# A projection stage with split fp32r products instead of fp32 ones, and the top-k selection spread along it

## Chip, cores and metric

One core of one Trainium2 chip runs the whole program in one launch. The metric is the device time of one execution in microseconds (us). "PE" is TensorE, "DVE" VectorE, "ACT" ScalarE, "POOL" GpSimd, and "SP" the queue that issues the DMAs.

## The reference, cut to what matters

Two request groups (1024 prompt frames and 32 sample frames, 1056 tokens in all) pass through two layers. Each layer normalises x, projects it with one wide `w_in`, runs four attention groups (sb, df, ds, fx), an output projection and a gated MLP with a depthwise convolution. The change is in the input projection and in what chooses the keys of the sparse group ds:

```python
hn = rmsnorm(x, g_mix)
parts = split_proj(jnp.einsum('btd,dn->btn', hn, w_in))      # 1024 -> 12 x 256 (q, k, v of 4 groups), 8*64 + 64 + 8 index columns, 4 gates
s_ix  = relu(einsum('bqhd,bkd->bqhk', q_ix, k_ix) * 64**-0.5)  # 8 index heads, one shared index key
score = einsum('bqh,bqhk->bqk', w_ix * 8**-0.5, s_ix)
score = where(chunk_ok, score, -inf)
top_val, top_idx = lax.top_k(score, topk)                      # topk = 256 for the prompt, 40 for the sample
logf  = log_sigmoid(parts[15] + b_forget);  c_all = cumsum(cat(plogf, logf))
```

The k and v rows, the index keys and `logf` are also outputs.

## The kernel before

Everything is a hand-written schedule: each stage is a `phase` in which five engine programs run side by side, tied by counted semaphores, and all engines meet at a barrier at its end. SBUF is one tensor, `arena`, that stages carve up anew. A loop over the two layers runs the stages in this order: norm, project the index columns, project the groups and select, attend, norm with the output projection in it, MLP.

**Norm** (`stage_norm`). xT holds x feature-major, 8 chunks of 128 features by 1056 tokens, and the norm goes in three pieces of 352 tokens. Called for the projection it writes the normalised values to hT by 24 DVE operations (line 565). Called with `split=True` (so far only ahead of the MLP) it writes them to a ring, ACT rounds each to fp32r (line 456), and DVE subtracts the rounded value to get the rest (line 534): `h_split` then holds a high and a low part.

**Index projection** (`stage_project_index`). For each of 9 token tiles (8 of 128 and one of 32) PE multiplies hT by the 584 index columns (line 650, plain fp32), ACT copies the result, PE turns it to feature-major (line 641) and DVE keeps it as qixT and kixT (lines 685, 687). kixT holds the shared key twice, with zeros in the other 64 rows, so that one product with all 128 rows picks one head of a pair.

**Projection and selection** (`stage_project_select`). 36 tiles (4 groups, GROUP_ORDER, by 9 token tiles) of 768 or 772 columns: products at line 883, ACT's copy to `nat` (line 942), the turns of q and k (line 898), their scaled copies (lines 952, 953) and the stores. Beside it, for the sample block (160 keys, "block 8") and the six prompt blocks with 384 to 1024 keys ("blocks 2 to 7"; the two smaller ones need no selection), PE makes the index scores of a head (line 907, two PSUM banks in turn), ACT applies the relu (line 969, a ring of 6), DVE multiplies by the head's weight and adds (lines 1012, 1014), masks the last tile of keys (line 1019) and then takes the largest 8 and marks them, 32 times in a row (5 for the sample; lines 1022, 1023). A last operation turns the marks into flags times 1e30 (line 1026). `projection_plan` puts the scores of a block among the tiles: `part 0` (the first 6 units) about one tile ahead, `part 1` when the block is due. Since each engine runs its program in order, PE, ACT and SP all follow that one list.

At block 5 stands the cumulative sum of the gates (`gates`, lines 991 and 996), for which PE turns the log gates (line 923).

**Attend** reads the flags as an fp32r operand of a product that adds them to the logits (line 1269), and starts with the queries and keys that the stage before wrote to DRAM (`q_turned`, `k_turned`).

Of the kernel before, what the change touches and what calls it, by code (L numbers as in the profile page):

```python
# [25 lines left out]
Unit = namedtuple("Unit", "v st heads map0 last")  # L26
Turn = namedtuple("Turn", "i kind of a t0 tiles eng nth")
# [23 lines left out]
RELU_RING = 6  # L51
# [15 lines left out]
WIDTH = dict(sb=3 * GW, df=3 * GW, ds=3 * GW, ix=NIX * HD + HD + NIX, fx=3 * GW + NH)  # L67
MIX = dict(sb=0, df=2, ds=4, fx=6)
W_OUT_SLOT = dict(ds=0, df=1, fx=0, sb=1)
PROJ = COL["fx"] + WIDTH["fx"]  # L70
# [13 lines left out]
BLOCKS = query_blocks()  # L84
TILES = [(i, i * P, P) for i in range(NT)] + [(NT, SEQ, DEC_SEQ)]
# [55 lines left out]
def place(nc):  # L141

    m = Memory()
    w_words = KC * WIDTH["fx"]
# [29 lines left out]
    m.stage_q, e = at(r0 + 4 * TOK, 2, 2 * P)  # L174
    m.stage_k, e = at(e, 2, 2 * P)
    assert e <= r0 + 6 * TOK
    m.qixT, e = at(r1, 4, TOK)
    m.kixT, e = at(e, 2, KEYS)
    m.relu, e = at(e, RELU_RING, BANK)
    m.nat, e = at(e, 3, WIDTH["fx"])  # L180
    m.cold, e = at(e, 2, GW)
    m.crow, e = at(e, KEYS)
    m.w_group = []
    for i in range(2):
        m.w_group.append(arena[:, total - (2 - i) * w_words:total - (1 - i) * w_words])
    assert e <= total - 2 * w_words
# [35 lines left out]

    m.ident_r, o = own_tensor("ident_r", F32R, o, P)
    m.mask_r, o = own_tensor("mask_r", F32R, o, 2, P)
    n_rows = sum(blk.keys for blk in BLOCKS[:NT] if blk.keys > TOPK_PROMPT)
# [37 lines left out]
    m.top = sb("top8", P, 8)  # L263
    m.ps = nc.alloc_psum_tensor("psum", [P, 8 * BANK], F32)
# [331 lines left out]
def load_w_in(m, a, l, g, slot):  # L596

    def load(sp, sem):
        w = m.w_group[slot][:, 0:KC * WIDTH[g]].rearrange("p (c n) -> p c n", c=KC)
        src = a["w_in"][l].rearrange("(c p) n -> p c n", p=P)  # L600
        for c in range(0, KC, 2):
            sp.dma_start(w[:, c:c + 2, :], src[:, c:c + 2, COL[g]:COL[g] + WIDTH[g]]).then_inc(sem, 16)
        return 16 * KC // 2
    return load

def stage_project_index(nc, m, a, l, load):  # L610
    n_w = WIDTH["ix"]
    w = m.w_group[0][:, 0:KC * n_w].rearrange("p (c n) -> p c n", c=KC)
    k0 = NIX * HD
    names = ["proj_done", "nat_ready", "weights_kept", "turned", "kept", "stored0", "stored1", "stored2",
             "cache_in", "next_in", "zeroed"]
    with phase(nc, *names) as s, nc.Block() as block:
        stored = [s.stored0, s.stored1, s.stored2]

        @block.sync
        def _(sp):  # L620
            for r in range(2):
                sp.dma_start(m.cold[:, 0, r * HD:(r + 1) * HD], a["cache_dsa_kidx"][l, 0]).then_inc(s.cache_in, 16)
            n_next = load(sp, s.next_in)
            for i, c0, n in TILES:
                sp.wait_ge(s.nat_ready, i + 1)
                dst = a["p_dsa_kidx"][l, 0, c0:c0 + n, :] if i < NT else a["s_dsa_kidx"][l, 0]
                sp.dma_start(dst, m.nat[0:n, i % 3, k0:k0 + HD]).then_inc(stored[i % 3], 16)
            for r in range(3):
                sp.wait_ge(stored[r], 16 * 3)
            sp.wait_ge(s.next_in, n_next)  # L630

        @block.tensor
        def _(pe):
            def turn(i, src, n):

                if i >= 2:
                    pe.wait_ge(s.kept, i - 1)
                for j in (range(5) if i <= NT else [4]):
                    o = (4 + 2 * (i % 2)) * BANK + j * P
                    col = j * P if i <= NT else 0  # L640
                    ins = nc.tensor.transpose(m.ps[:, o:o + n], src[0:n, col:col + P], m.ident[0:n, 0:n])
                ins.then_inc(s.turned, 1)

            for i, c0, n in TILES:
                if i >= 2:
                    pe.wait_ge(s.nat_ready, i - 1)
                for c in range(KC):
                    for n0, n1 in ((0, BANK), (BANK, n_w)):
                        o = (i % 2) * 2 * BANK
                        ins = nc.tensor.matmul(m.ps[0:n, o + n0:o + n1], m.hT[:, c, c0:c0 + n], w[:, c, n0:n1],  # L650
                                               start=(c == 0), stop=(c == KC - 1))
                ins.then_inc(s.proj_done, 1)
                if i >= 1:
                    pe.wait_ge(s.nat_ready, i)
                    turn(i - 1, m.nat[:, (i - 1) % 3, :], TILES[i - 1][2])
            pe.wait_ge(s.nat_ready, NT + 1)
            turn(NT, m.nat[:, NT % 3, :], DEC_SEQ)
            pe.wait_ge(s.cache_in, 32)
            turn(NT + 1, m.cold[:, 0, :], P)

        @block.scalar
        def _(act):
            for i, c0, n in TILES:
                act.wait_ge(s.proj_done, i + 1)
                if i >= 3:
                    act.wait_ge(s.turned, i - 2)
# [12 lines left out]
        def _(dve):  # L679
# [18 lines left out]
            keep(NT + 1, P)  # L698

def taken_rows(m):

# [1228 lines left out]
```

## Time and profile before

| | us |
|---|---|
| median of 3 runs | 3880.66 |
| lowest, highest | 3869.41, 3881.22 |
| the profiled execution | 3867.68 |
| its span, first to last instruction | 3865.9 |
| PE, DVE, ACT, POOL busy in the span | 3574.3, 2486.4, 1065.8, 34.4 |
| from the first load of the norm stage to the next stage (layer 0) | 63.9 to 95.1 |
| index projection (layer 0) | 95.1 to 182.7 |
| projection and selection (layer 0) | 182.7 to 664.1 |

The stage times are read from the timeline: a stage begins where all engines start again after the barrier. PE's busy time counts pipelined products to their modelled ends, so a high share alone does not say that PE is the bound. Layer 1 repeats the same stages with almost the same lengths (index projection 1977.3 to 2062.9, selection from 2065.8).

### The profile page before, as it was taken

Reading aid. Unit: us, or ns where it says so; the run is one execution under the profiler, and the core shown is the slowest. Engines: PE = TensorE matmul, PEld = TensorE weight load, DVE = VectorE, ACT = ScalarE, POOL = GpSimd, SP = SyncE. Lnnn points to the kernel's source line nnn. Section 1 sums busy time; section 2 is a strip of 40 time slices with the busy share of each in tenths; the row PEclk is TensorE's granted clock in tenths of the full one; section 3 lists DMA queues with packets and bytes.
Section 4 is the critical chain, followed back from the end, with each engine's and each line's share of the span. In section 5 each row is a group of like instructions: output and inputs, shape, how many; then the busy total and the mean of one; then the engine's idle time right before and its main releaser. Section 6 shows DMA issues by size and latency. Waiting matters only on the chain. (4 is left out here: it accounts for less than half of the span.)

```text
span 3865.9 us, 53489 instructions
## 1 busy us (share of the span) xinstructions
PE 3574.3 (92%) x19553; PEld 2728.9 (71%) x19553; DVE 2486.4 (64%) x4584; ACT 1065.8 (28%) x2223; POOL 34.4 (1%) x160
## 2 busy tenths in 40 slices
PE   3999999999979999999969999989899799999995
PEld 2554555655659999999935555555566699999994
DVE  3188996575754666656635899947655566665665
ACT  3111211565632111111111111245654311111112
POOL 0000000000000000000000000000000000000000
PEclk7999999998989999999989999999999899999997
DMA  4212213211002111111011112141100111111101
GB/s 165 71 37 68 68 38 110 69 57 50 21 12 61 49 49 34 47 49 49 12 63 56 65 41 73 41 145 61 48 12 23 44 50 49 33 48 49 49 28 46
DMA packets 216658, 206.69 MB, mean 53 GB/s; under 512 B 23846, under 2 KB 193158, under 8 KB 214430
## 3 DMA queue, kind: packets, MB, share of 16 engines
q1 hardware_dynamic: 216478, 204.36, 16.4%
q8 instruction: 104, 1.70, 0.2%
q14 instruction: 76, 0.62, 0.1%
HBM read 159.41 MB, written 44.91 MB: 53 GB/s over the span
## 5 line engine op out<-in xcount | busy, mean ns | idle before, releaser
L1624 PE MATMUL psum<-h_split,gate_up_split 128*128 128x352 f32 x6336 | 1019.2, 322 | 44.1 <-DVE gate_up_split L1738 44.1
L1624 PEld LDWEIGHTS psum<-h_split,gate_up_split 128*128 128x128 f32 x6336 | 1011.2, 188 | 48.3 <-issue 46.8
L883 PE MATMUL psum<-arena 128*128 128x512 f32 (+4 forms) x2304 | 756.9, 487 | 0.0
L1768 DVE TENSOR_TENSOR arena<-arena,psum 128x352 f32<-128x352 f32 x1056 | 513.6, 521 | 318.3 <-PE psum L1624 318.2
L883 PEld LDWEIGHTS psum<-arena 128*128 128x128 f32 (+1 forms) x2304 | 413.5, 181 | 329.8 <-issue 291.3
L1624 PE MATMUL psum<-hid_split,down_split 128*128 128x352 f32 x3168 | 523.1, 325 | 11.1 <-DVE down_split L1738 11.1
L1624 PEld LDWEIGHTS psum<-hid_split,down_split 128*128 128x128 f32 x3168 | 516.6, 190 | 11.6 <-issue 11.6
L1022 DVE MAX8 top<-arena 128x8 f32<-128x384 f32 (+6 forms) x394 | 346.6, 880 | 13.5
L1023 DVE MATCH_REPLACE8 arena<-top,arena 128x384 f32<-128x384 f32 (+6 forms) x394 | 339.1, 861 | 0.0
L1496 DVE CUSTOM_DVE_ANT_0 arena<-psum,arena 128x128 f32<-128x128 f32 (+8 forms) x288 | 198.0, 703 | 200.6 <-PE psum L1259 89.9
L1709 ACT CAST hid_split<-hidden 128x1056 fp32r<-128x1056 f32 x44 | 47.3, 1076 | 834.5 <-DVE hidden L1753 834.5
L1124 PE MATMUL psum<-arena 128*128 128x352 f32 x768 | 260.7, 483 | 2.3 <-PEq L124 2.3
L1259 PE MATMUL psum<-arena 64*128 64x512 f32 (+9 forms) x1040 | 217.6, 522 | 38.5 <-DMA arena<-q_turned 17.9
L942 ACT COPY arena<-psum 128x768 f32<-128x768 f32 (+3 forms) x72 | 57.5, 798 | 690.0 <-PE psum L883 690.0
L1306 PE MATMUL psum<-const_tile,arena 128*128 128x128 f32 (+1 forms) x1216 | 199.4, 284 | 20.7 <-DVE arena L1567 8.4
L1415 ACT ACTIVATE arena<-arena,row_mins 128x128 f32<-128x128 f32 (+8 forms) x288 | 210.1, 731 | 3.5 <-DVE row_mins L1496 3.5
L1124 PEld LDWEIGHTS psum<-arena 128*128 128x128 f32 x768 | 142.2, 195 | 89.6 <-issue 19.3
L1306 PEld LDWEIGHTS psum<-const_tile,arena 128*128 128x128 f32 (+1 forms) x1216 | 140.0, 142 | 92.2 <-issue 40.0
L1386 ACT COPY arena<-psum 128x512 f32<-128x512 f32 (+4 forms) x312 | 142.7, 474 | 199.5 <-PE psum L1306 198.0
L1322 PE MATMUL psum<-arena 128*64 128x128 f32 (+1 forms) x2432 | 178.1, 283 | 0.9 <-ACT arena L1389 0.9
L650 PE MATMUL psum<-arena 128*128 128x512 f32 (+3 forms) x576 | 160.6, 439 | 15.3 <-PEq L124 15.3
L907 PE MATMUL psum<-arena 128*128 128x512 f32 (+4 forms) x352 | 150.2, 567 | 17.0 <-ACT arena L969 12.2
(139 smaller groups left out, 2677.9 us busy)
## 6 DMA issues: line engine op xcount, KB each, us to landing
gate_up_raw<-in_w_gate SPq DMA_DIRECT2D x44, 512.0 KB, 3.6
gate_up_raw<-in_w_up SPq DMA_DIRECT2D x44, 512.0 KB, 4.7
down_raw<-in_w_down SPq DMA_DIRECT2D x44, 512.0 KB, 3.5
arena<-in_w_in SPq DMA_DIRECT2D x24, 768.0 KB, 7.0
arena<-k_turned SPq DMA_DIRECT2D x8, 1184.0 KB, 5.6
k_turned<-arena SPq DMA_DIRECT2D x72, 128.0 KB, 2.2
q_turned<-arena SPq DMA_DIRECT2D x64, 128.0 KB, 2.1
arena<-bias_strips SPq DMA_DIRECT2D x4, 2048.0 KB, 10.0
```

The source lines that it names most:

```text
L650: ins = nc.tensor.matmul(m.ps[0:n, o + n0:o + n1], m.hT[:, c, c0:c0 + n], w[:, c, n0:n1], start=(c == 0), stop=(c == KC - 1))
L883: ins = nc.tensor.matmul(m.ps[0:n, o + n0:o + n1], m.hT[:, c, c0:c0 + n], w[:, c, n0:n1], start=(c == 0), stop=(c == KC - 1))
L1022: own(nc.vector.max(m.top[0:blk.rows, :], score))
L1023: own(nc.vector.match_replace(out=score, in_to_replace=m.top[0:blk.rows, :], in_values=score, imm_value=TAKEN))
L1124: ins = nc.tensor.matmul(out[:, 0:PIECE], m.w_out[W_OUT_SLOT[g]][:, k, c * P:(c + 1) * P], m.mix[:, MIX[g] + k, p * PIECE:(p + 1) * PIECE] ...
L1259: ins = nc.tensor.matmul(S(x0 + c)[0:n, k0:k1], m.q_ring[f, st.e % 3, st.hp, 0:n], m.kT[slot][f, st.hp, blk.key0 + k0:blk.key0 + k1], star ...
L1306: ins = nc.tensor.transpose(PT(t.i)[0:kn, i * P:i * P + n], prob(x)[0:n, k0:k0 + kn], m.ident[0:n, 0:n])
L1322: ins = nc.tensor.matmul(O(st.e)[a * HD:(a + 1) * HD, st.hp, 0:n], m.v[SLOT[st.g]][0:kn, vt, col:col + HD], m.probT[0:kn, (st.j % 2 * 2 + ...
L1415: nc.scalar.activation(p, p, ACT.Exp, bias=m.low[0:n, x % PROB_RING:x % PROB_RING + 1], scale=-1.0, accum_out=m.sums[0:n, st.e % 2, col:co ...
L1496: nc.vector.tensor_tensor_reduce(out=prob(x)[0:n, 0:blk.keys], in0=S(x)[0:n, 0:blk.keys], in1=bias, scale=1.0, scalar=3e38, op0=ALU.add, o ...
L1624: ins = nc.tensor.matmul(out, w[i], x[k], start=(first and n == 0), stop=(last and n == 2))
L1768: nc.vector.tensor_tensor(x, x, bank(m, down_bank[p])[:, 0:PIECE], ALU.add).then_inc(s.added, 1)
```

## The change

The two projection stages become one, `stage_project`, and the norm ahead of it is called with `split=True`. `w_in` is cut into 15 pieces: one "special" (index key, index weights, gates; 128 columns wide with padding), two "index" (256 columns of index queries each) and q, k, v of each group (256 columns each). ACT rounds a piece to fp32r (`high`), POOL subtracts (line 993, `low`). Each product is three fp32r products (high x high, high x low, low x high). Special, index and q pieces are made feature-major, 352 tokens at a time (24 products of 352 columns each, line 857), so they need no turn; k and v pieces token-major (24 products of 256 columns each, line 855). An output uses one of 4 PSUM banks. kixT has the key in both halves, and a score product takes 64 rows, the lower half for even heads and the upper for odd ones (line 893). The relu ring has 4 units. `ProjectPlan` puts scores among outputs by its own clock, `now`, and by `block_time`. The scores of a block go key range by key range, no longer head by head. Flags stay 0 or 1, the factor 1e30 moves to the identity of the attention, and finished rows of all blocks but the last are copied to their place by DMA at the stage's end.

The core of the diff:

```diff
-RELU_RING = 6
+RELU_RING = 4
+def block_time(blk):
+    rounds = (TOPK_PROMPT if blk.n < NT else TOPK_SAMPLE) // ROUNDS_OF_8
+    return rounds * (2 * (blk.keys / 960 + 0.14) + 0.09) + 2 * NIX * (blk.keys / 960 + 0.1) * 0.7
+    def lay_out(self, waiting):
+        plan, now, due, begun = self.plan, 0.0, 0.0, False
+        for o in self.outs:
+            p = o.piece.i
+            if o.o == self.first_out(p):
+                plan.append(("piece", o.piece))
+                if p == 3:
+                    due = now
+            if p >= 3:
+                if waiting and not begun and now >= due - 8:
+                    self.begin(waiting[0])
+                    begun = True
+                while waiting and now >= due:
+                    blk = waiting.pop(0)
+                    if blk.n == GATES_BLOCK:
+                        plan.append(("gates", blk))
+                    plan.append(("score", (blk, 1)))
+                    begun = False
+                    due = max(due, now) + block_time(blk)
...
+            plan.append(("out", o))
+            now += 3.75 if o.piece.kind not in "kv" else 2.8
...
+        def _(sp):
+            for what, x in plan.plan:
+                if what == "piece" and x.i + 1 < len(pieces):
+                    p = x.i + 1
+                    sp.wait_ge(s.high, p)
+                    sp.wait_ge(s.low, p)
+                    load_piece(m, a, l, pieces[p])(sp, s.raw_in)
+                if what == "out":
+                    sp.wait_ge(s.kept, x.o + 1)
...
+            def out(o):
+                if o.o >= OUT_RING:
+                    pe.wait_ge(s.kept, o.o - OUT_RING + 1)
+                if o.o == plan.first_out(pc.i):
+                    pe.wait_ge(s.high, pc.i + 1)
+                    pe.wait_ge(s.low, pc.i + 1)
...
+                    for n, (i, k) in enumerate(((0, 0), (0, 1), (1, 0))):
+                        if pc.kind in "kv":
+                            ins = nc.tensor.matmul(dst[:, 0:GW], m.h_split[:, k, c, t0:t0 + P], w[i][:, c, :], start=start, stop=stop)
+                        else:
+                            ins = nc.tensor.matmul(dst[:, 0:PIECE], w[i][:, c, o.f * P:(o.f + 1) * P],
+                                                   m.h_split[:, k, c, o.c0:o.c0 + PIECE], start=start, stop=stop)
...
+            def high(p):
+                n = KC * pieces[p].width
+                if p:
+                    act.wait_ge(s.raw_in, raw_count(p))
+                if p >= 2:
+                    act.wait_ge(s.proj_done, plan.last_out[p - 2] + 1)
+                nc.scalar.copy(m.w_split[p % 2][:, 0, 0:n], m.w_raw[:, 0:n]).then_inc(s.high, 1)
+            def piece(pc):
+                if pc.i + 1 < len(pieces):
+                    high(pc.i + 1)
...
+            for pc in pieces:
+                pool.wait_ge(s.high, pc.i + 1)
+                nc.gpsimd.tensor_tensor(w[:, 1, 0:n], m.w_raw[:, 0:n], w[:, 0, 0:n].bitcast(F32), ALU.subtract).then_inc(s.low, 1)
```

The list orders PE, ACT and SP alike. Three places of it matter below. First PE's program at the head of the stage. Before (the last turns of the index projection, then scores and the first tile; line 907 is a score, line 883 a product of a tile):

```order
L641 MATMUL psum<-const_tile,arena 128x32 x5
L641 MATMUL psum<-const_tile,arena 128x128
L616 UNCONDITIONAL_BRANCH
L872 UNCONDITIONAL_BRANCH
L907 MATMUL psum<-arena 32x160 x8
L907 MATMUL psum<-arena 128x384 x6
L883 MATMUL psum<-arena 128x512
L883 MATMUL psum<-arena 128x260
```

Now (line 857 is a feature-major product of special, index or q, 24 to an output; 867 and 871 are turns; 893 is a score):

```order
L857 MATMUL psum<-h_split,w_in_split_50 128x352 x72
L857 MATMUL psum<-h_split,w_in_split_51 128x352 x24
L867 MATMUL psum<-const_tile,arena 128x128 x8
L867 MATMUL psum<-const_tile,arena 32x128
L871 MATMUL psum<-const_tile,arena 128x128
L857 MATMUL psum<-h_split,w_in_split_51 128x352 x120
L857 MATMUL psum<-h_split,w_in_split_50 128x352 x144
L893 MATMUL psum<-arena 32x160 x8
L893 MATMUL psum<-arena 128x384 x4
L857 MATMUL psum<-h_split,w_in_split_51 128x352 x48
L893 MATMUL psum<-arena 128x384 x4
```

The scores of block 8 now stand behind 15 outputs of the one stage, and the second part of block 2 behind two more.

Second, PE's program at the end of the stage. Before, with the second part of block 7 between two tiles and nine more tiles behind it:

```order
L883 MATMUL psum<-arena 32x256
L898 MATMUL psum<-const_tile,arena 128x128 x4
L907 MATMUL psum<-arena 128x512 x10
L883 MATMUL psum<-arena 128x512
L883 MATMUL psum<-arena 128x256
```

Now, with the last value outputs (line 855 is a k or v product) and then the 16 scores of block 7 as the last thing that PE does:

```order
L880 MATMUL psum<-const_tile,arena 128x32 x2
L880 MATMUL psum<-const_tile,arena 128x128 x2
L855 MATMUL psum<-w_in_split_50,h_split 128x256 x192
L893 MATMUL psum<-arena 128x512 x16
L756 UNCONDITIONAL_BRANCH
```

All outputs now stand ahead of block 7's scores.

Third, ACT's program around the second part of block 5. Before, between two tiles (942 copies a tile, 952 and 953 the turned q and k, 969 is a relu):

```order
L942 COPY arena<-psum 128x772
L952 ACTIVATE arena<-psum 128x256
L953 COPY arena<-psum 128x256
L969 ACTIVATE arena<-psum 128x512 x6
L942 COPY arena<-psum 128x772
L952 ACTIVATE arena<-psum 128x256
L953 COPY arena<-psum 128x256
L969 ACTIVATE arena<-psum 128x512 x2
```

Now (924 rounds the next piece of weights once its load has landed, 945 and 940 copy outputs, 977 is a relu, 968 a turned k):

```order
L945 ACTIVATE arena<-psum 128x352
L977 ACTIVATE arena<-psum 128x512 x4
L945 ACTIVATE arena<-psum 128x352
L924 CAST w_in_split_51<-w_in_raw 128x2048
L940 COPY arena<-psum 128x256
L977 ACTIVATE arena<-psum 128x512 x4
L977 ACTIVATE arena<-psum 128x256 x8
L940 COPY arena<-psum 128x256
L968 COPY arena<-psum 128x256
```

The rounding of the next piece, which waits for a load, now stands ahead of outputs and of relus in ACT's order. (The rows of before are those of block 3, which has the same form.)

## Rows read from the trace of the kernel before

**Rows 1.** Busy by stage, layer 0: PE, PEld, DVE, ACT, POOL; then clock, DMA share, GB/s.

```profile
63.90:95.10 31.20, 5.06 (x8) 1.92 (x8) 23.59 (x52) 14.50 (x34) 0.01 (x1) 0.50 0.25 83
95.10:182.70 87.60, 84.91 (x334) 47.18 (x334) 11.98 (x38) 6.82 (x18) 2.07 (x1) 0.97 0.12 40
182.70:664.10 481.40, 464.33 (x1490) 254.42 (x1490) 416.29 (x695) 92.38 (x204) 1.88 (x10) 0.98 0.21 68
```

**Rows 2.** Timeline, DVE and PE, both ends of the selection stage: start, length, operation, idle before.

```profile
184.34 0.29 DVE L1012 TENSOR_SCALAR arena<-arena,index_weights 32x160 f32<-32x160 f32 x1 [2.35 <-ACT arena L969]
...
643.48 0.69 DVE L1026 TENSOR_SCALAR taken_keys<-arena 128x1024 fp32r<-128x1024 f32 x1
...
644.79 0.60 PE L898 MATMUL psum<-const_tile,arena 128*128 128x128 f32 x4
...
645.32 10.51 PE L883 MATMUL psum<-arena 128*32 128x512 f32 x32
...
656.80 0.88 PE L898 MATMUL psum<-const_tile,arena 32*128 32x32 f32 x6 [0.38 <-ACT arena L942]
666.57 1.22 PE L1259 MATMUL psum<-arena 64*128 64x128 f32 x8 [8.89 <-DMA arena<-q_turned]
```

**Rows 3.** Groups by line and form, DVE, 184.34 to 644.17: busy, mean ns, idle before.

```profile
L1022 DVE MAX8 top<-arena 128x8 f32<-128x1024 f32 x32 | 39.3, 1227 | 1.1
L1023 DVE MATCH_REPLACE8 arena<-top,arena 128x1024 f32<-128x1024 f32 x32 | 38.7, 1209 | 0.0
...
L1014 DVE SCALAR_TENSOR_TENSOR arena<-arena,index_weights 128x512 f32<-128x512 f32 x42 | 31.2, 748 | 17.9 <-ACT arena L969 16.7
...
L1022 DVE MAX8 top<-arena 128x8 f32<-128x384 f32 x32 | 17.9, 561 | 1.1
L1023 DVE MATCH_VALUE_LOAD arena<-top,arena 128x8 f32 x192 | 17.7, 92 | 6.6
L1023 DVE MATCH_REPLACE8 arena<-top,arena 128x384 f32<-128x384 f32 x32 | 17.4, 543 | 0.0
```

**Rows 4.** Timeline, DVE, additions of block 7.

```profile
551.58 1.61 DVE L1014 SCALAR_TENSOR_TENSOR arena<-arena,index_weights 128x512 f32<-128x512 f32 x2 [2.46 <-ACT arena L969]
553.40 1.61 DVE L1014 SCALAR_TENSOR_TENSOR arena<-arena,index_weights 128x512 f32<-128x512 f32 x2 [0.20 <-ACT arena L969]
```

**Rows 5.** Groups by line, whole span: the split products of the MLP.

```profile
L1624 PE MATMUL psum<-h_split,gate_up_split 128*128 128x352 f32 x6336 | 1019.2, 322 | 44.1 <-DVE gate_up_split L1738 44.1
```

**Rows 6.** Timeline, DVE: the end of the norm before the projection, and of the split norm.

```profile
85.80 8.02 DVE L565 SCALAR_TENSOR_TENSOR arena<-arena,state_and_gains 128x352 f32<-128x352 f32 x16
...
1150.19 0.57 DVE L565 SCALAR_TENSOR_TENSOR norm_ring<-arena,state_and_gains 128x352 f32<-128x352 f32 x1
...
1151.12 0.57 DVE L565 SCALAR_TENSOR_TENSOR norm_ring<-arena,state_and_gains 128x352 f32<-128x352 f32 x1
```

**Rows 7.** Groups by line, whole span: casts on ACT, subtractions on DVE.

```profile
L1738 DVE TENSOR_TENSOR gate_up_split<-gate_up_raw,gate_up_split 128x2048 fp32r<-128x2048 f32 x44 | 100.9, 2293 | 35.2 <-ACT gate_up_split L1702 35.2
...
L1702 ACT CAST gate_up_split<-gate_up_raw 128x2048 fp32r<-128x2048 f32 x44 | 83.8, 1905 | 24.3 <-DMA gate_up_raw<-in_w_up 15.6 <-PEq L124 8.6
```

**Rows 8.** DMA issues: size of one, median us from issue to landing.

```profile
arena<-in_w_in SPq DMA_DIRECT2D x24, 768.0 KB, 7.0
...
arena<-in_w_out SPq DMA_DIRECT2D x8, 1024.0 KB, 5.1
```

**Rows 9.** Timeline, the gates at block 5.

```profile
375.45 0.20 DVE L991 SCALAR_TENSOR_TENSOR forget_rows<-forget_temps 128x36 f32<-128x36 f32 x1
...
379.98 0.71 DVE L1012 TENSOR_SCALAR arena<-arena,index_weights 128x512 f32<-128x512 f32 x2
```

**Rows 10.** Groups by line, POOL, whole span.

```profile
L676 POOL MEMSET arena<- 128x2368 f32 x2 | 4.1, 2072 | 174.4 <-POOLq L124 174.4
```

More of the change, by code:

```diff
@@ L727, in taken_keys @@
     return out
-GROUP_ORDER = ["fx", "ds", "df", "sb"]
+PROJECT_ORDER = ["fx", "ds", "df", "sb"]
 GROUP_ROW = dict(sb=0, df=1, ds=2, fx=3)
 GATES_BLOCK = 5
-def projection_plan(blocks):
-    tiles, jobs, plan = [], [], []
-    for gi, g in enumerate(GROUP_ORDER):
-        for i, c0, n in TILES:
-            tiles.append((gi, g, i, c0, n))
-    waiting, due, begun = list(blocks), 0.0, False
-    for t, (gi, g, i, c0, n) in enumerate(tiles):
-        if waiting and not begun and t >= due - 1:
-            plan.append(("score", (waiting[0], 0)))
-            begun = True
-        while waiting and t >= due:
-            blk = waiting.pop(0)
-            if blk.n == GATES_BLOCK:
-                plan.append(("gates", blk))
+SPECIAL = HD + NIX + NH
@@ new lines, in begin, with turn @@
+    def begin(self, blk):
+        us = []
+        for k0 in range(0, blk.keys, BANK):
+            for h in range(NIX):
+                us.append((self.n_units, h, k0, min(k0 + BANK, blk.keys)))
+                self.n_units += 1
+        self.units[blk.n] = us
+        self.plan.append(("score", (blk, 0)))
+    def turn(self, o, g=None):
+        if o is None:
+            t = Turned(len(self.turns), g, None, NT + 1, 0, P)
+        else:
+            t = Turned(len(self.turns), o.piece.of, o, o.i, o.c0, o.n)
+        self.turns.append(t)
+        self.plan.append(("turn", t))
@@ new lines, with stage_project, raw_count, w_split @@
+PROJECT = ProjectPlan(SELECTED)
+def stage_project(nc, m, a, l, d, outs, caches, load):
+    plan = PROJECT
+    pieces, proj = plan.pieces, plan.outs
+    index_done = plan.last_out[2] + 1
+    rows = score_rows(m)
+    names = ["raw_in", "high", "low", "proj_done", "kept", "stored0", "stored1", "stored2", "moved0", "moved1",
+             "cold_in", "turned", "turn_kept", "staged0", "staged1", "keys_ready", "taps_ready", "weights_kept",
+             "scored", "relu_done", "added", "dve_steps", "act_steps", "softened", "logf_done", "logf_turned", "scanned",
+             "cache_gates_in", "gates_kept", "spread", "crow_out", "selected", "taken_out", "next_in"]
+    with phase(nc, *names) as s, nc.Block() as block:
+        stored, moved, staged = [s.stored0, s.stored1, s.stored2], [s.moved0, s.moved1], [s.staged0, s.staged1]
+        key_turns = [t for t in plan.turns if t.of not in ("special", "index keys")]
+        def raw_count(p):
+            return 16 * sum(len(pc.columns) for pc in pieces[1:p + 1])
+        def w_split(p):
+            w = m.w_split[p % 2][:, :, 0:KC * pieces[p].width]
+            return [w[:, i, :].rearrange("p (c n) -> p c n", c=KC) for i in range(2)]
@@ L972, in _ @@
             act.preload_act_table_set("natural_log_exp_and_others")
[L973 removed]
+            high(0)
+            for what, x in plan.plan:
                 if what != "gates":
[L975 removed]
+                    {"piece": piece, "out": out, "turn": turn, "score": score}[what](x)
         @block.gpsimd
```

535 lines of the change are left out of this document (252 added, 283 removed).

## The prediction

> **What bounds the kernel now.** I read the busy times by stage first. The two projection stages take 87.6 + 481.4 = 569.0 us in each layer [rows 1]. In the second both PE (464 busy) and DVE (416) are nearly full, and the granted clock is 0.98. So the next question is who ends last, and the timeline answers it: DVE's chain runs from 184.34 to 643.48 + 0.69 = 644.2, PE's last product follows at 657.7, and the next stage's first product comes at 666.57 after a wait for q_turned [rows 2]. The DVE groups say what the 459.8 us of that chain are: a round of 1024 keys is 1227 + 1209 + 92 ns and the gaps, 2.58 us, 32 times; with 384 keys 561 + 543 + 92, 1.25 us; so about 1.04 ns per key and operation. Ready additions of 512 keys step at about 0.855 us (1.61 for two, overlapping, 1.81 with the wait) [rows 3, 4]. Idle time before them is small: 17.9 us before the 512-key additions, for relus [rows 3]. So before, selection is the chain from 184 on, and PE runs 13 us behind it at the end: the stage is balanced. In the index stage PE is alone (84.9 of 87.6 busy, DVE 12) [rows 1]; nothing of the selection can start there.
>
> The sum is made against the profiled execution, 3867.7 us with a span of 3865.9. The median of the runs is 3880.7, 13 us higher; I add that at the end.
>
> **Norm.** 24 subtractions are added on DVE, which is what the stage ends on (23.6 busy of 31.2, all work at the end is DVE's) [rows 1, 6]. A scaled chunk alone steps at 8.02 / 16 = 0.50 us, a scaled chunk with its subtraction at 1151.12 - 1150.19 = 0.93 [rows 6]. 24 x 0.43 = **+10.3 us** per layer. ACT's 24 roundings go beside it.
>
> **What a product costs.** The nearest split products, 352 columns in the MLP, take 1019.2 / 6336 = 0.161 us each [rows 5], 0.457 ns per column. A plain fp32 product has two passes: 32 passes of 512 and 256 columns took 10.51 us [rows 2], 0.855 ns per column and pass, so half of it, 0.428, is the lower end for a one-pass product. For 352 columns: 0.150 to 0.161, I take 0.161 (same form, same tensors). For 256 columns no row exists: 0.109 (half a plain pass) to 0.161 (no gain from fewer columns); I take the rate of the 352-column ones, 0.117 [rows 5]. An output of 24 products then costs 3.86 us (special, index, q) or 2.80 (k, v).
>
> **Head of the stage, to DVE's first addition.** Start-up and table 1.6 (182.7 to 184.3) [rows 2], of which 1.3 precede the rounding; rounding of the small first piece 1.0, half of 1905 ns [rows 7]; then POOL's subtraction of 1024 columns. POOL's rate for two inputs is not in the trace: 0.875 ns per column is its fill [rows 10], three times that (two reads, one write) 2.6, so 0.9 to 2.7 here and 1.8 to 5.4 for a full piece; DVE needs 2.29 for a full piece [rows 7]. I take 2.2 here and 4.4 for a full piece; the end of the range costs 1 us, since a piece lasts over 22. Products begin at 4.5. The Trainium skill, GPSIMD Engine Reference, section 3.1 (elementwise cycle accounting), puts a two-input operation of 2048 elements at 4497 ns on GpSimd against 2293 on VectorE; the trace has the second number exactly, none of the first.
>
> Three special outputs 11.6, plus 2.6 for the clock: the norm runs at a granted 0.50, and the index stage's mean of 0.97 over 87.6 us is 2.6 us lost at its start [rows 1]; PE is as idle before the new stage. Output 4: 3.9. Now ACT must round piece 2 before it may copy output 4 or the turns. SP issues that load only after the special outputs are kept (about 19), 1 MB lands after 5.1, as the one of in_w_out does, [rows 8], the cast takes 1.9 [rows 7]: ACT is free at 26.5, so PE waits about 4 and the ten turns, each with its copy, take 3. Eleven outputs: 42.5. Then PE may score, but ACT first has to round piece 4: 0.4 + 5.1 + 1.9 = 7.4 before the first relu, and 0.7 for it. Sum 4.5 + 14.2 + 3.9 + 7 + 42.5 + 8.1 = **80.2**. Before, the first addition came 184.34 - 95.1 = 89.2 after the index stage began. So the head gains 9, less than the norm loses.
>
> **From there to block 6.** After the first addition PE makes the rest of block 8, four units of block 2 and two q outputs (3.5 + 2.6 + 7.7, begun 0.7 earlier): **13**. Up to block 6's second part its list then holds 78 outputs: 22 of 3.86 = 84.9 and 56 of 2.80 = 156.8. To them come 31 turns of two transposes, 0.60 / 2 + 0.03 = 0.33 each [rows 2], 10.2; scores, which PE in its order can only make as fast as relu ring and additions take them: 28 of 512 keys at 0.89, 4 of 384 at 0.72, 8 of 256 at 0.58, 8 of 128 at 0.45 = 36.0 (a bare 512-key score is two passes, 0.87 by the rate above); the gates 379.98 - 375.45 = 4.5 [rows 9]; and the holds of ACT at a piece's start (7.4 us, of which the 4 banks cover 4 x 2.80 = 11.2 unless scores or turns stand there): 0 to 24, I take 8. Sum **300**.
>
> DVE needs in that time, for blocks 2 to 5: rounds 32 x (1.25 + 1.52 + 1.78 + 2.05) = 211, additions 34.5, masks and flags 3, gates 4.5: 253. So PE is the bound there, by 47 us, and DVE waits at the start of blocks 3, 4, 5 and 6. The planner's clock `now` counts outputs alone (3.75 and 2.8), neither turns nor scores, so its due times do not see this.
>
> **The end.** Behind the mark of block 6 DVE has 11 of additions, 0.3 + 74.2 + 0.65 for mask, rounds and flags; then block 7, whose relus are ready: 16 x 0.855 = 13.7, 0.3, 82.6, 0.7. Sum **183.5**; PE's last 16 outputs (45) and turns lie under it. The loads of the next stage and the copies of flags lie under block 7's 82.6. Barrier 1.5, an estimate (no stage before ends without a tail of its own). Before, PE's 13 us and the stores behind it lay here; that tail is gone.
>
> **Sum.** 80.2 + 13 + 300 + 183.5 + 1.5 = 578 against 569.0, +9; with the norm +19.5 per layer, **+39** for both. 3867.7 + 39 = 3907, and on the scale of the median 3920. Attention has the same products (the factor is moved), and four small ACT operations more at its start, nothing against its 420.
>
> The scores in array halves: the two banks are freed one after the other by relus of 0.6 us, so two scores rarely run together. Each saves at most a part of 0.87 where DVE's 0.855 step rules. 0 to -3 per layer; I take 0.
>
> **Rivals.**
> *Selection covers everything (faster).* If PE gets from block 2's mark to block 6's in DVE's 253 instead of 300, the stage is 531 and a layer -27.5: 3867.7 - 55 = 3813, 3826 on the median's scale. For it: PE has a third fewer product columns to stream (three passes for four). Against it: that is counted above; PE would have to be 16% cheaper than the rows, and even the lower end of the product prices gives 7%. Chance 0.10.
> *One-pass products at the plain rate (no change).* With 0.150 and 0.109 the head saves 4, the stretch 5.8 + 10.8: -20.6 per layer, sum 0: 3866, 3879 on the median's scale. Against it: 6336 products of the MLP at 0.161. Chance 0.14.
> *k and v products no cheaper than those of 352 columns (much slower).* Each loads its own weights for 256 columns only. 56 x 24 x 0.044 = +59 per layer: 4038. Against it: two transposes with their own loads cost 0.3. Chance 0.05.
> *POOL blocks DVE.* The additions read two SBUF operands while POOL subtracts. If a DVE operation waits out a whole subtraction each time, 1.8 to 5.4 for each of 14: but up to block 6 DVE has 47 us to spare, and only pieces 13 and 14 fall near the mark of block 6 or behind it, so at most 2 x 5.4 per layer, +22: 3942. Nothing in the trace speaks to it, POOL being idle. Chance 0.06, inside the forecast's side. The Trainium skill, SBUF — State Buffer, section "Who interferes with whom", has this rule: a DVE instruction with two SBUF inputs contends with a GpSimd one that reads SBUF, and the second to issue is blocked. No row here shows it.
> *Longer holds.* With the 7.0 us of the in_w_in loads [rows 8] each hold grows by 1.9; three in the head and about four uncovered ones give +13 per layer: 3946. Chance 0.10, part of the same side.
>
> **Numbers.** The forecast with its variants (holds, POOL) has 0.71 and its own range is 3895 to 3950. About 0.3% (11.6 us) is what a measurement of this kernel tells from no change. Slower by more 0.74 (with the dear products, less the forecast's lower edge), same 0.14, faster 0.12. The range 3868 to 3955 leaves out the full gain and the dear products.
>
> **What would show it.** In the changed profile: 24 more DVE operations in the norm and a stage 10 us longer; first addition near 80 us after the stage's start, with ACT waiting for a load ahead of the first relu; products of 256 columns at 0.117; waits of DVE for relus at the start of blocks 3, 4, 5 and 6, 10 or so each, none at block 7, where PE waits for relus instead; PE idle for the last 85 us; the selection stage some 578 long. I am wrong if DVE is without waits from block 3 on, if the 256-column step is near 0.109 or 0.161, or if rounds of MAX8 lengthen while POOL works.

## The result, and the profile after

The changed kernel takes 3987.6 us (median of 4 runs), the kernel before 3875.0 in the same session: ratio 1.0294, 95% interval 1.0273 to 1.0314, slower. The forecast had slower, by 39 us; it is 113. The profiled executions are 3989.0 and 3867.7, 121 apart.

The windows by stage, as in [rows 1] (norm, then the one projection stage from barrier to barrier):

```profile
63.90:106.20 42.30, 5.06 (x8) 1.91 (x8) 34.03 (x76) 24.52 (x58) 0.00 (x0) 0.50 0.10 16
106.20:717.20 611.00, 459.60 (x2940) 410.33 (x2940) 437.69 (x701) 126.99 (x268) 66.80 (x18) 0.83 0.20 66
```

The norm grew by 42.3 - 31.2 = 11.1 us, the stage from 569.0 to 611.0. That is 53 us per layer, 106 of the 121 between the two profiles. The rest is small: attention and MLP take what they took, but for the second layer's attention, 401 us here from its first score product to its last against 390.5 in the profile of before. All 12 experiments below have 400 to 405 there, and so has the first layer's in both kernels; the 390.5 is that one profile's, and no step of the change explains it. The runs of the kernel before fall into two groups, 3867 to 3873 and 3876 to 3884 us, its profile is of the lower one, and the 10.6 us of that attention are about what parts the groups, though no run shows that it is the cause.

PE is busy for less than before (459.6 against 549.2 in both stages of before), and still the stage is longer; its granted clock is 0.83. The timeline at the marks of the forecast (first addition, part two of block 2, part two of block 6, the last flags, the next stage), which answer to [rows 2]:

```profile
187.48 4.36 DVE L1049 TENSOR_SCALAR arena<-arena,index_weights 32x160 f32<-32x160 f32 x1 [51.42 <-ACT arena L977]
...
206.78 0.92 PE L893 MATMUL psum<-arena 64*128 64x384 f32 x4
...
526.24 1.13 PE L893 MATMUL psum<-arena 64*128 64x512 f32 x4
...
715.71 0.69 DVE L1023 TENSOR_SCALAR taken_keys<-arena 128x1024 fp32r<-128x1024 f32 x1
...
719.73 1.23 PE L1294 MATMUL psum<-arena 64*128 64x128 f32 x8 [88.47 <-DMA arena<-q_turned]
```

Subtracting them gives the table; the last column is the sum's error, 33 us per layer.

| stretch | forecast | measured | over |
|---|---|---|---|
| stage start to first addition | 80.2 | 81.3 | 1.1 |
| to part two of block 2 | 13 | 19.3 | 6.3 |
| to part two of block 6 | 300 | 319.5 | 19.5 |
| to the last flags' end | 183.5 | 190.2 | 6.7 |
| to the barrier | 1.5 | 0.8 | -0.7 |

The groups by line of the stage (busy, mean ns, idle before), beside [rows 3, 5, 8]:

```profile
L855 PE MATMUL psum<-w_in_split,h_split 128*128 128x256 f32 x1728 | 224.8, 291 | 0.0
...
L893 PE MATMUL psum<-arena 64*128 64x512 f32 x96 | 44.8, 838 | 31.7 <-ACT arena L977 31.1 <-DVE arena L1013 0.6
L1051 DVE SCALAR_TENSOR_TENSOR arena<-arena,index_weights 128x512 f32<-128x512 f32 x42 | 40.5, 964 | 39.4 <-ACT arena L977 36.0
L1021 DVE MAX8 top<-arena 128x8 f32<-128x1024 f32 x32 | 39.3, 1228 | 1.1
...
L924 ACT CAST w_in_split<-w_in_raw 128x2048 fp32r<-128x2048 f32 x14 | 26.7, 1905 | 81.9 <-DMA w_in_raw<-in_w_in 81.9
```

MAX8 is as before (1228 ns against 1227 [rows 3]). A 512-key addition takes 964 ns in the mean, against 748. ACT waits 81.9 us for weights, 5.85 per piece. Three places of the timeline show three different things. First, an addition of 160 keys, 0.3 us before, takes 4.36 and ends 0.09 us after POOL's subtraction beside it; the relu, then PE, stand behind it:

```profile
187.25 4.50 POOL L993 TENSOR_TENSOR w_in_split<-w_in_raw,w_in_split 128x2048 fp32r<-128x2048 f32 x1 [18.18 <-ACT w_in_split L924]
...
191.93 0.29 ACT L977 ACTIVATE arena<-psum 32x160 f32<-32x160 f32 x1 [3.26 <-DVE arena L1049]
...
192.28 5.47 PE L893 MATMUL psum<-arena 64*32 64x160 f32 x12 [2.81 <-ACT arena L977]
```

Second, at a k piece's start ACT waits for a load, then casts, and PE's turn stands behind it (a "hold" below); the output after that takes 4.62 instead of the 3.0 of the one ahead:

```profile
226.19 0.39 SPq L738 DMA_DIRECT2D w_in_raw<-in_w_in  x1
...
227.79 3.01 PE L855 MATMUL psum<-w_in_split,h_split 128*128 128x256 f32 x24
231.29 1.90 ACT L924 CAST w_in_split<-w_in_raw 128x2048 fp32r<-128x2048 f32 x1 [5.69 <-DMA w_in_raw<-in_w_in]
...
233.60 0.41 PE L880 MATMUL psum<-const_tile,arena 128*128 128x128 f32 x2 [2.81 <-ACT arena L940]
233.77 4.62 PE L855 MATMUL psum<-w_in_split,h_split 128*128 128x256 f32 x24
```

Third, the granted clock (third column from the end) in three runs of scores (part two of blocks 5, 6 and 7), and in the one output that follows block 4's scores:

```profile
423.40:437.50 14.10, 11.79 (x25) 5.55 (x25) 12.73 (x15) 6.31 (x13) 4.50 (x1) 0.50 0.07 13
526.20:539.50 13.30, 12.14 (x25) 5.23 (x24) 8.27 (x10) 5.82 (x12) 3.86 (x1) 0.57 0.09 31
616.00:631.40 15.40, 13.96 (x20) 4.99 (x20) 10.38 (x16) 6.66 (x12) 0.00 (x0) 0.50 0.00 1
...
345.70:350.90 5.20, 5.20 (x27) 5.20 (x27) 4.88 (x10) 0.28 (x1) 0.00 (x0) 0.53 0.00 0
```

0.5 is 1.2 GHz: scores of 64 rows run at half speed, and so does the output behind them, 5.2 us for 24 products that take 2.9 to 3.1 elsewhere. The selection stage of before, with scores of 128 rows, has 0.98 [rows 1].

So four causes were on the table: POOL blocks DVE, late loads, the clock in score runs, and the place of the scores in PE's order.

### The profile page after: what moved, and what is told of

It reads as the page before. It is cut to its first block and busy times, and to the rows that moved or that the text cites. A ratio compares the mean times of both kernels' runs of the same rounds, so it can differ in the third digit from the quotient of the medians.

```text
span 3987.2 us, 58145 instructions
## 1 busy us (share of the span) xinstructions
PE 3411.5 (86%) x21785; PEld 2957.4 (74%) x21785; DVE 2525.9 (63%) x4568; ACT 1141.9 (29%) x2365; POOL 160.1 (4%) x174
## 5 line engine op out<-in xcount | busy, mean ns | idle before, releaser
L1660 PE MATMUL psum<-hid_split,down_split 128*128 128x352 f32 x3168 | 523.8, 325 | 11.1 <-DVE down_split L1774 11.1
L855 PE MATMUL psum<-w_in_split,h_split 128*128 128x256 f32 x3456 | 449.8, 291 | 0.0
L855 PEld LDWEIGHTS psum<-w_in_split,h_split 128*128 128x128 f32 x3456 | 436.5, 197 | 9.9 <-issue 9.9
L857 PE MATMUL psum<-h_split,w_in_split 128*128 128x352 f32 x1872 | 313.7, 330 | 46.0 <-POOL w_in_split L993 46.0
L857 PEld LDWEIGHTS psum<-h_split,w_in_split 128*128 128x128 f32 x1872 | 309.5, 194 | 54.3 <-issue 54.3
L1294 PEld LDWEIGHTS psum<-arena 64*128 64x128 f32 (+3 forms) x1040 | 88.6, 192 | 273.4 <-DMA arena<-q_turned 180.1
L893 PE MATMUL psum<-arena 64*128 64x512 f32 (+4 forms) x352 | 148.4, 746 | 90.3 <-ACT arena L977 87.2
```

Of the source, the lines that this page charges most:

```text
L855: ins = nc.tensor.matmul(dst[:, 0:GW], m.h_split[:, k, c, t0:t0 + P], w[i][:, c, :], start=start, stop=stop)
L857: ins = nc.tensor.matmul(dst[:, 0:PIECE], w[i][:, c, o.f * P:(o.f + 1) * P], m.h_split[:, k, c, o.c0:o.c0 + PIECE], start=start, stop=stop)
L893: nc.tensor.matmul(bank(m, 6 + x % 2)[0:blk.rows, 0:k1 - k0], m.qixT[f, h // 2, blk.q0:blk.q0 + blk.rows], m.kixT[f, blk.key0 + k0:blk.key ...
L1294: ins = nc.tensor.matmul(S(x0 + c)[0:n, k0:k1], m.q_ring[f, st.e % 3, st.hp, 0:n], m.kT[slot][f, st.hp, blk.key0 + k0:blk.key0 + k1], star ...
L1660: ins = nc.tensor.matmul(out, w[i], x[k], start=(first and n == 0), stop=(last and n == 2))
```

## The experiments

Times are medians; ratios are to the kernel before, run beside them, with their 95% intervals. The change itself is at 3987.6 and 1.0294. Differences below are of the medians. The median of the kernel before moved between 3870 and 3880 from session to session, and the ratios move with it: e2 and e7 have the same median and ratios 0.25% apart. No variant was measured in two sessions, so a difference of a few us between sessions tells nothing.

| run | edit | us | ratio |
|---|---|---|---|
| e1 | POOL subtracts 16 columns from piece 3 on; the other low halves are left out | 3974.2 | 1.0271 (1.0254 to 1.0288) |
| e10 | POOL's subtraction in eight | 3976.5 | 1.0242 (1.0218 to 1.0267) |
| e2 | scores over 128 rows; the separation of the heads is left out | 3953.8 | 1.0219 (1.0202 to 1.0236) |
| e7 | keys zero-padded, 128 rows | 3953.7 | 1.0194 (1.0173 to 1.0215) |
| e8 | scores in a row in one half | 4007.8 | 1.0334 (1.0313 to 1.0355) |
| e3 | loads early | 3927.1 | 1.0147 (1.0130 to 1.0164) |
| e4 | planner's costs raised | 3923.3 | 1.0138 (1.0121 to 1.0155) |
| e5 | e3 + e4 + e10 | 3866.2 | 0.9970 (0.9960 to 0.9980) |
| e6 | e5 + e7 | 3846.3 | 0.9918 (0.9897 to 0.9938) |
| e9 | e6, costs higher still | 3876.6 | 0.9997 (0.9986 to 1.0008) |
| e12 | e6, one wait of DVE later | 3822.2 | 0.9852 (0.9833 to 0.9871) |
| e11 | e9, the same wait later | 3821.4 | 0.9853 (0.9834 to 0.9873) |

**POOL and DVE (e1, e10).**

```diff
-                n = KC * pc.width
+                n = KC * pc.width if pc.i < 3 else 16
```

> From piece 3 on POOL subtracts only 16 of 2048 columns, so the low halves of those weights are left out (stale values are multiplied in their place); PE, ACT, DVE and all loads are as in the change. The stage from the barrier to the next barrier takes 611 us in the change. POOL theory (a DVE addition or flag pass that starts while POOL subtracts ends only with it, 3 to 5 us each at 187, 269, 325, 424 and 526 us, and PE stands behind it, since its scores wait in order for relus and those for additions): DVE's additions all take 0.35 to 0.75 us, PE's gaps of 2 to 3 us inside score runs go, the stage is 10 to 16 us shorter, 3988 becomes 3956 to 3968. Clock theory (scores of 64 rows let the granted clock fall, and that costs the time): clock stays near 0.9 in the stage and 3983 to 3988. Load theory (PE waits for ACT, ACT for its load): 3985 to 3988. List theory (part two of each block stands too late in PE's order): 3985 to 3988.

Measured: 13 us less (9 by the ratios), short of the 20 to 32 that the POOL theory asked for, and more than the others allow. All the long additions are gone. Its group and POOL's in the stage:

```profile
L1051 DVE SCALAR_TENSOR_TENSOR arena<-arena,index_weights 128x512 f32<-128x512 f32 x42 | 31.6, 752 | 43.9 <-ACT arena L977 40.9
...
L993 POOL TENSOR_TENSOR w_in_split<-w_in_raw,w_in_split 128x16 fp32r<-128x16 f32 x12 | 2.6, 220 | 376.2 <-ACT w_in_split L924 376.2
```

The mean is 752, close to the 748 before the change. In the profiled layer DVE is busy for 16.4 us less (421.3 against 437.7) and the stage is 6.3 us shorter, so POOL's subtraction does hold up DVE, and more than half of that is covered.

e10 keeps the work and cuts the instruction:

```diff
+                for c in range(8):
+                    k = slice(c * n // 8, (c + 1) * n // 8)
+                    ins = nc.gpsimd.tensor_tensor(w[:, 1, k], m.w_raw[:, k], w[:, 0, k].bitcast(F32), ALU.subtract)
+                ins.then_inc(s.low, 1)
```

> The change with POOL's subtraction in eight instructions, nothing else (and nothing left out). In e5, where both are in, a DVE addition beside such a row took 1.03 us and the two engines went turn by turn. POOL theory: no addition over 1.2 us, the waits of e1 gone but for 0.3 to 0.5 us per addition: as e1, 3974 to 3980. Rival (what e1 gained came from its short low halves, which were there earlier for PE): no gain, 3985 or more.

It gains what e1 gains (11 us; 20 by the ratios), so e1's gain did not come from low halves that were there earlier. A DVE operation now waits out one piece of POOL's and POOL waits for it in turn. In the timeline of e5, which has the same edit, six additions, which step at 0.855 when ready, stand at 1.07 each, and seven pieces, which step at 0.70 in e10 where DVE is idle, at 0.97:

```profile
372.41 6.80 POOL L1000 TENSOR_TENSOR w_in_split<-w_in_raw,w_in_split 128x256 fp32r<-128x256 f32 x7
...
374.21 6.40 DVE L1059 SCALAR_TENSOR_TENSOR arena<-arena,index_weights 128x512 f32<-128x512 f32 x6
```

**The clock (e2, e7, e8).** e2 changes one slice:

```diff
-                    f = slice(h % 2 * HD, h % 2 * HD + HD)
+                    f = slice(0, P)
```

> Each score product reads all 128 rows instead of its 64, so the scores are sums over two heads: what is left out is the separation of the heads; number, columns and order of all instructions are those of the change. Clock theory (products of 64 rows count as little activity, the granted clock falls to 1.2 GHz in score runs and the first output behind them runs at half speed): granted clock of the stretch 526 to 539.5 rises from 0.58 to above 0.9, the output behind block 4's scores goes from 5.3 to 2.9 us, block 7's additions from 16.6 to about 14 us; 8 to 12 us per layer, 3988 becomes 3964 to 3972. POOL, load and list theories: the clock falls because PE stands idle between scores, so it falls again; and two scores no longer run beside each other: 3985 to 3995.

Measured: 34 us less, more than the theory's 16 to 24. e7 has 128 rows and keeps the heads apart; `special` becomes the first of two copies of the keys, zero in rows 64 to 127, and `kixT` the second, zero in rows 0 to 63:

```diff
-                    f = slice(h % 2 * HD, h % 2 * HD + HD)
-                    nc.tensor.matmul(bank(m, 6 + x % 2)[0:blk.rows, 0:k1 - k0], m.qixT[f, h // 2, blk.q0:blk.q0 + blk.rows],
-                                     m.kixT[f, blk.key0 + k0:blk.key0 + k1], start=True, stop=True).then_inc(s.scored, 1)
+                    keys = m.kixT if h % 2 else m.special
+                    nc.tensor.matmul(bank(m, 6 + x % 2)[0:blk.rows, 0:k1 - k0], m.qixT[:, h // 2, blk.q0:blk.q0 + blk.rows],
+                                     keys[:, blk.key0 + k0:blk.key0 + k1], start=True, stop=True).then_inc(s.scored, 1)
```

> The change with the two zero-padded copies of the keys alone: scores of 128 rows, right ones, two scores no longer beside each other in the array. If e2's gain of 31 us came from the rows of the product (clock), this has the same less 1 or 2 us per layer for DVE's fills in the head: 3954 to 3962. If it came from the values in e2 (larger sums, other data), the gain is absent: 3985 or more.

> Heads in the order 0 2 4 6 1 3 5 7, so that scores in a row use the same half of the array; 64 rows as in the change, nothing left out. Clock theory by rows: the granted clock stays low in score runs (0.5 to 0.6 from 526 to 539.5 us), and two scores no longer share the array, so a score of 512 keys takes two passes of 0.86 alone: 3995 to 4015. Rival: it is the interleaving of two scores in halves that the clock answers to: it stays at 1, 3955 to 3970. If neither matters: 3984 to 3990.

Measured: e7 34 us less than the change, e8 20 us more. The runs of scores of block 5's and block 6's part two, windows of e7, and then of e8, where block 7's follows:

```profile
417.30:430.80 13.50, 10.20 (x26) 4.78 (x27) 12.24 (x14) 6.45 (x13) 4.50 (x1) 0.87 0.07 12
517.20:528.60 11.40, 11.36 (x28) 4.75 (x27) 8.67 (x11) 6.19 (x12) 3.94 (x1) 0.85 0.11 36
```

```profile
427.20:441.40 14.20, 13.02 (x25) 5.95 (x25) 12.83 (x15) 6.41 (x13) 4.50 (x1) 0.55 0.07 13
529.90:545.90 16.00, 15.94 (x26) 6.68 (x25) 8.87 (x11) 6.20 (x13) 3.86 (x1) 0.53 0.08 26
621.00:639.40 18.40, 16.07 (x20) 5.68 (x20) 11.80 (x17) 6.57 (x11) 0.00 (x0) 0.50 0.00 0
```

In e8, PE is busy for 15.94 of 16.00 us and still gets 0.53; in e7 it is as busy (11.36 of 11.40) and gets 0.85, though it had stood for 3.1 us just before and in e8 for 2.7. So it is not idleness between scores that lowers the clock, nor the alternation of halves, but that the products have 64 rows: same columns, same count, half the rows. This holds for stretches that have nothing else. In the attention of the change, products of 64 rows (line 1294) stand eight in a row among others of 128, and there the clock is 1.00:

```profile
739.70:759.70 20.00, 19.34 (x168) 13.46 (x168) 10.66 (x29) 10.87 (x27) 0.00 (x0) 1.00 0.26 73
```

e8 also shows what the halves are worth: block 6's run takes 16.0 us when they share one half against 13.3 when they alternate, so two scores do overlap, at 1.2 GHz. With 128 rows it takes 11.4. The halves save a part of the work and lose more by the clock.

**The loads (e3).**

```diff
-                if what == "piece" and x.i + 1 < len(pieces):
-                    p = x.i + 1
+                if what == "piece" and x.i == 0:
...
+                    p = x.piece.i + 2
+                    if x.o == plan.first_out(x.piece.i) + 2 and p < len(pieces):
+                        sp.wait_ge(s.high, p)
+                        sp.wait_ge(s.low, p)
+                        load_piece(m, a, l, pieces[p])(sp, s.raw_in)
```

> The load of piece p+1 is issued by SP behind the third output of piece p-1 (its staging tile is free since POOL's subtraction), not behind the last. Load theory: ACT no longer waits 5.4 to 7.7 us for w_in_raw ahead of its rounding; the gaps of PE at the turns of the head (4.3), before block 8's relus (7.3), at 230.8, 322.4 and 523.1 (2.8 to 2.9 each, and 1.5 of the next output) fall to under 1: 9 in the head and 6 to 11 behind it, 15 to 20 per layer, 3988 becomes 3948 to 3958. If DVE or the order of the list set the time instead, the head gives its 9 and the rest nothing: 3968 to 3974.

Measured: 60 us less (57 by the ratios), more than expected (30 to 40). The waits of ACT in e3's stage, beside the 81.9 of the change:

```profile
ACT w_in_split L928 <- DMA w_in_raw<-in_w_in: 12.6, 2, 7.5
```

The stage of the profiled layer is 27 us shorter. 5.4 of them lie ahead of the first addition, where 9 were expected; the surplus is behind it. Each hold of PE had also cost the low speed of the output after it (4.62 above), and POOL's subtractions now come where DVE selects: of four additions over 1 us per layer one is left. So e3 takes away most of what e1 does as well, and its 60 us are not the loads' alone.

**The order (e4).**

```diff
+                    now += 0.9 * len(self.units[blk.n])
...
-            now += 3.75 if o.piece.kind not in "kv" else 2.8
+            now += dict(k=3.6, v=3.2).get(o.piece.kind, 4.2)
```

> Only the planner's costs: 4.2, 3.6 (k) and 3.2 (v) us per output, and 0.9 for each score when part two is placed. Block 6's part two then stands behind 83 outputs instead of 95, block 5's behind 63 instead of 70, block 7's behind 106 instead of 111. List theory (DVE waits at the starts of blocks 3 to 6 because scores stand behind too many outputs): 12 outputs fewer ahead of block 6, 12 x 2.9 = 35 us; DVE's last operation 25 to 35 us earlier per layer, 3988 becomes 3918 to 3938. POOL, clock and load theories: the waits are not the order's, the stage gains less than 10 per layer, 3968 or more.

Measured: 64 us less (61 by the ratios), as the list theory said. Waits of DVE in its stage: 45.6 us for relus before L1051 became 21.8, but a new line appeared, whose meaning I only saw at e9:

```profile
DVE arena L1052 <- ACT arena L978: 21.8, 13, 6.8
...
DVE top L1022 <- PE psum L856: 12.5, 1, 12.5
```

**Together (e5, e6), too far (e9), and the last wait (e11, e12).**

> The early load of e3, the planner's costs of e4, and POOL's subtraction cut into eight pieces of 256 (128 for piece 0) columns each, about 0.6 us long; nothing left out. If the three causes lie one behind the other (each takes its own waits away), the gains add: 57 + 61 + 10 = 128 us and 3988 becomes 3856 to 3872, about the time of the kernel before. If they hide one another (a wait that one removes was only the cover of the next), no more than the larger two thirds: 3885 or more. With pieces of 0.6 us no DVE addition takes over 1.4 us if a blocked operation waits for one POOL instruction only; if POOL's pieces follow so closely that DVE is let in only after the last, additions of 4 us stay.

> As e5, and the keys in two copies with the other half zero, so that each score product has 128 rows (right scores; nothing left out), for one 1184-column and one 1184-column fill more on DVE in the head. Clock theory: as e2 against the change, 10 to 17 us per layer less than e5, as far as DVE is not the bound by then: a DVE chain without waits would be 81 - 5 + 448 us, a stage of some 530; 3825 to 3850, faster than before by about 1%. Rival: with part two placed early PE waits anyway and the clock is no longer on the path: within 5 us of e5.

Both came out inside their ranges: 3866 and 3846. The stage of the profiled layer is 27.2, 31.1 and 5.8 us shorter in e3, e4 and e10, 64 together, and 65 in e5 (by the medians 136 and 122 for the whole kernel): these three add up, or nearly. The padded keys do not: they gave 34 us alone and 20 on top of e5. e6 beats the kernel before.

> e6 with the planner's costs raised further (4.5, 3.8 for k, 3.4 for v, 1.0 per score): block 7's part two stands behind 101 outputs instead of 106, block 6's behind 79 instead of 83, block 5's behind 60 instead of 63. In e6 DVE still loses some 11 us at block 7 (108.8 from its first addition to block 6's flags against 97.6 without waits) and 5 at block 4. List theory: those go, 8 to 14 us per layer, 3846 becomes 3818 to 3832. Rival: scores placed too early make PE wait for the ring of relus while DVE still selects, and the outputs come later; then 3840 to 3852, with PE's idle time ahead of scores growing from about 7 us to 20 and more.

This fell outside both: 3877, slower than e6 by 30 us. The timeline of e9 at block 7:

```profile
580.86 1.23 DVE L1031 MAX8 top<-arena 128x8 f32<-128x1024 f32 x1 [27.71 <-PE psum L860]
```

DVE stands for 27.7 us, between block 7's last addition and its first MAX8, for PE's last product: the code waits there because block 7's flags go into the space of the split inputs. Only the flags need it, the selection writes over the scores. The more outputs stand behind block 7's scores, the longer it waits, and in the change, where none does, it costs nothing. In e6 it costs 12.4 us. The edit:

```diff
             def select(blk, score, flags):
...
+                if blk is SELECTED[-1]:
+                    dve.wait_ge(s.proj_done, len(proj))
                 nc.vector.tensor_scalar(flags, score, TAKEN / 2, None, ALU.is_gt).then_inc(s.selected, 1)
...
                 if blk is SELECTED[-1]:
-                    dve.wait_ge(s.proj_done, len(proj))
                     flags = taken_keys(m)[blk.n]
```

> e9 with one wait moved: DVE waits for PE's last product right before it writes block 7's flags into the space of the split inputs, not before block 7's first MAX8. In e9 DVE stood there for 27.7 us (PE's last ten outputs), in e6 for 12.4. Theory that this wait is why e9 lost against e6: the whole 27.7 goes, the products lie under the selection, and 3877 becomes 3818 to 3826, below e6. Rival (e9 lost because PE waits in the ring of relus): the wait only moves behind the selection, 3865 or more.

> e6 with the same wait moved: 12.4 us per layer go, 3846 becomes 3820 to 3826. With the wait out of the way e11 and e12 differ only by the place of the scores: if DVE's chain is now without waits in both, they agree within 5 us. If nothing is gained, DVE's wait in e6 was covered by something else that ends later: 3840 or more.

3821 and 3822, as expected and equal: the place of the scores no longer matters, and the ring of relus, e9's rival, cost nothing that shows. The stage of e12, from barrier to barrier, and the longest waits of DVE from 181 us on:

```profile
107.00:634.80 527.80, 438.41 (x2940) 396.07 (x2940) 430.38 (x702) 131.04 (x273) 84.58 (x123) 0.92 0.24 76
```

```profile
DVE arena L1062 <- ACT arena L984: 39.8, 1, 39.8
...
DVE arena L1023 <- PE psum L912: 3.0, 2, 2.5
...
DVE arena L1064 <- ACT arena L984: 2.5, 2, 2.4
```

After the first addition (the 39.8 lie ahead of it) DVE waits 5.5 us in these rows. The stage takes 527.8 against 569.0: nearly without waits of DVE, it reaches the 531 of the forecast's first rival, though by other edits than that rival supposed. That is 41 us per layer, less the norm's 11, or 60 in all; by the medians the kernel is 57 us faster than the one before, 1.5%.

## Why the forecast was wrong

The direction and the chain were right: products of 256 columns cheaper than those of 352, PE the bound ahead of block 6, DVE behind it, the norm on the path. The size was wrong by 74 us, 33 per layer in the stage: the sum took scores of 64 rows at full clock, took a hold of PE for no more than its gap, and let POOL block DVE at no cost up to block 6. By its own steps:

- **Norm +10.3:** 11.1, right.
- **What a product costs:** 0.161 and 0.117 us were taken. Eight v outputs in a row (467.85 to 490.75 us) step at 2.86 us, forecast 2.80; k outputs with their turn at 3.07, forecast 3.13; those of 352 columns at 3.86, as forecast. Near enough; the rivals of other product prices fall.
- **Head 80.2:** 81.3, right.
- **"A bare 512-key score is two passes, 0.87 by the rate above", and halves "0 to -3".** The first step that failed. The rate was that of tile products with 128 rows at full clock [rows 2]; the clock of products with 64 rows was in no row, and I did not give it a bound. It costs 34 us in all, by the medians (e2, e7), in the scores, in block 7's additions (16.6 us; forecast 13.7, and 14.0 in e7) and in the outputs behind.
- **"The holds of ACT ... 0 to 24, I take 8".** There are three gaps of 2.8 to 2.9 us at the turns in the stretch, 8.5 together, so the 8 was right for the gaps alone. Missing was the half speed behind them (4.6 us for an output in place of 3.1, after two of the three). That loads are late was counted (4 and 7.4 in the head, where 4.1 and 7.0 were measured), but not that it is SP's order alone that makes them so: the load issued at 226.19 us goes to a tile that had been free since POOL's subtraction ended at 191.75.
- **"Up to block 6 DVE has 47 us to spare"**, so POOL may block it at no cost. Another wrong step: DVE's slack is no cover, as PE's scores wait in order for the relus, and these for the additions. At 187 us the addition's extra 4.1 us made 2.8 of PE's. It costs 11 to 13 us in all (e10, e1). What the rival said of DVE holds: an addition or flag pass that starts beside a subtraction lasts until that ends (five per layer: four additions and one flag pass). The Trainium skill, SBUF — State Buffer, section "Who interferes with whom", has also the case that I left out: an operation of one input in a two-port mode contends too. The 4.36 us and the flag pass of 4.17 are TENSOR_SCALARs of one input, so the trace agrees, as far as they ran in such a mode, which no row says.
- **Block 6 to the end 183.5:** 190.2, from the additions of block 6 (15.1 us where 11 were taken: low clock, and POOL from 525.56 to 530.06 us) and of block 7 (16.6 where 13.7 were taken). The MAX8 rounds are right. "None at block 7" is not quite: DVE does not wait at its start, but 4.1 us for relus between its additions, since the scores behind them run at 1.2 GHz.
- **The planner's clock** "counts outputs alone": right, and it was the largest cost that one edit took back (64 us, little more than e3's 60), but it was in the sum already as the 47 us of waits, and does not explain the error.

Do these make up the error? Per layer the clock is 17 us and POOL 6, by the medians of the runs that remove them. Of the holds, e3 took 21.8 us off the profiled layer behind the first addition, where the sum had 8: 13.8 more. Together that is 37, against the 33 that the stage was over, and it counts some things twice: e3 also moved POOL's work off the additions, and the low clock stands behind the holds too. So the three causes are shown, each by a run that removes it, and they are large enough; how the error divides among them exactly stays open.

## What to carry to other kernels

Before a product is split by rows, read the granted clock of a stretch that has only such products, or pad the rows with zeros: the padded form was faster here. Slack of one engine covers a delay only if no other engine waits for it in its own order. When work is reordered, look for a wait that guards a late write but stands ahead of long work: it costs nothing until the order changes.

## What the runs showed of the hardware

Stretches of 64-row products alone are granted 1.2 GHz even when PE is busy for 15.94 of 16.00 us (0.53; with zero rows added, 0.85 in the same run of scores), and the output behind them starts at that clock: 24 products took 5.2 us instead of 3.0. Among products of 128 rows, in attention, they ran at 1.00. Two products in different halves of the array do overlap: 13.3 against 16.0 us for block 6's part two. A TENSOR_SCALAR with one input in SBUF waited out POOL's whole subtraction (4.36 us for 160 keys). MAX8 and MATCH_REPLACE did not: those of 384 keys beside a subtraction took 0.56 and 0.54 us, their mean without one [rows 3]:

```profile
233.27 4.58 POOL L993 TENSOR_TENSOR w_in_split<-w_in_raw,w_in_split 128x2048 fp32r<-128x2048 f32 x1 [41.52 <-ACT w_in_split L924]
...
233.96 0.56 DVE L1021 MAX8 top<-arena 128x8 f32<-128x384 f32 x1
...
234.63 0.54 DVE L1022 MATCH_REPLACE8 arena<-top,arena 128x384 f32<-128x384 f32 x1
```

POOL's subtraction of 2048 columns took 4.57 us, the value that the forecast bounded by 1.8 and 5.4.
